# A mixture-of-experts layer: the partial job of an expert moves from first to second place, and the job table takes its sums in two wide operations

## The chip, the core and the metric

The kernel runs on one core of a Trainium2 chip. The metric is the device time of one execution in microseconds (us), over several executions. TensorE (PE in the profile) multiplies matrices, VectorE (DVE), ScalarE (ACT) and GpSimd (POOL) work elementwise, SyncE (SP) only issues transfers here. The engines run on their own and meet at semaphores.

## What is computed

One layer over 1024 latent tokens of width 1024, batch 1: modulation, an input projection, a recurrent head group and a linear-attention head group, an output projection, a normalisation, and then a mixture of 32 experts of which each token takes 4. The change lies in the experts' part. Cut to that, the reference is:

```python
logits = (xt @ w_router + b_router).astype(f32)          # 1024 tokens, 32 experts
top_v, top_i = lax.top_k(logits, 4)
top_w = jax.nn.softmax(top_v, axis=-1)
...
def expert_block(args):                                   # tokens of one expert
    tok, e = args
    xb = xt[tok]
    gate = jnp.minimum(xb @ w_gate[e] + b_gate[e], 7.0)
    up = jnp.clip(xb @ w_up[e] + b_up[e], -7.0, 7.0)
    act = (up + 1.0) * gate * jax.nn.sigmoid(1.702 * gate)
    return act @ w_down[e] + b_down[e]
...
y = jnp.zeros_like(xt).at[row_token].add(y_rows * row_weight)
x = layer_norm(DEEPNORM_ALPHA * x + g2 * y)
```

All is in float32. The weights of an expert are three matrices of 4 MB, 12 MB together; of 32 experts, 384 MB.

## The kernel before, in words

**Jobs.** The 4096 pairs of token and expert are cut, expert after expert, into jobs of at most 128 rows. An expert with NQ quarters of 32 rows has NJ = ceil(NQ / 4) jobs and PAD = 4 NJ - NQ quarters too many. One of its jobs is partial and has the kind 4 - PAD (1, 2 or 3 quarters); the others are of kind 4. The kernel decides this while it runs, from the router's result. It writes a table with one row for each job (lines 1748 to 1773): kind (J_TYP), expert, whether the job is the first of its expert (J_FIRST), and ordinals that say which count of a semaphore to wait for. The table goes to DRAM and back (lines 520 and 522), and every engine reads its rows into registers. Before, the partial job is the first of its expert. Line 1765 gives kind 4 to the very last job of all, whatever its padding, because the end of the kernel is written for that kind.

With the given inputs there are 49 jobs. The counts of matmuls in the timeline of TensorE and the times at which weights are loaded give their kinds, with a bar between experts: 4 4 | 3 | 2 4 | 2 4 | 3 | 1 4 | 2 | 3 | 2 4 4 | 1 | 3 | 2 | 2 4 | 1 | 3 | 4 | 3 | 2 4 4 | 1 4 | 4 | 3 | 3 | 2 | 1 4 | 1 4 4 | 4 | 1 4 | 4 | 4 | 2 4 | 2 4 | 1 4. Jobs are numbered from 0 to 48 and experts from 0 to 31. In the table, job n has row n + 1, and `uf` is the job's number.

**TensorE** (lines 574 to 626 and 964 to 989) runs gate and up of job n (line 586, 64 matmul records for each quarter, 32 columns of the array at a time), then the down projection of job n - 1, then gate and up of job n + 1, and so on. The down projection has a full sweep (line 612) for kind 4, a half sweep (616) for kind 2, a quarter sweep (622) for kind 1, and half and quarter for kind 3. A full sweep takes as long for 29 rows as for 128.

**Weights.** SBUF holds one set: gate and up as four pairs of pieces of 1 MB, down as four pieces. SyncE works through the jobs in order (lines 543 to 566). In its turn for job n it first, if job n + 1 opens an expert, waits until the biases of job n's expert are spread (`bias_spread`, by VectorE at the end of its turn for the job before, line 1703), then issues that expert's biases and its four pairs (line 501), each as soon as gate/up of job n has used the pair. Then, if job n opens an expert, it issues the down row and the down pieces (line 529) of job n's expert, each as soon as the down projection of job n - 1 has used the piece; in a kind-3 job that is in its quarter sweep, which comes last. All these transfers stand in one queue. So the next expert's gate/up weights are loaded from the time at which the expert's last job uses them, and are wanted after the down projection of the job before that one.

**VectorE**, in its turn for job n: it turns the rows of job n + 1 (line 1656), does the swiglu of job n (1684 to 1696), evacuates and weighs the down result of job n - 1 (1638, 1643), turns the activations of job n (1713), and spreads the next biases if an expert ends (1703). **GpSimd** gathers rows (2001) and adds the weighed results into `stream_rows` in DRAM by indirect DMAs (2015).

**The end.** The results of the last three jobs are fetched back separately (`late_rows`, line 2032) and normalised (lines 1669 and 1674), while all other rows are normalised during the last job. The fetch of the last two waits until all scatters before have landed.

Of the kernel before, what the change touches and what calls it, by code (L numbers as in the profile page):

```python
# [13 lines left out]
ALU = mybir.AluOpType  # L14
ACT = mybir.ActivationFunctionType
AX_X = mybir.AxisListType.X
# [4 lines left out]
P = 128  # L21
# [4 lines left out]
class Chain:  # L26
# [5 lines left out]
    def link(self, ins):  # L32
        self.n += 1
        ins.then_inc(self.sem, 1)
        self.eng.wait_ge(self.sem, self.n)


def layer(nc, x, c, ctx, c_ctx, w_ada, b_ada, w_in, conv_w, conv_b, lru_wa, lru_ba, lru_wx, lru_bx,
# [17 lines left out]
    NE, TOPK = w_router.shape[2], 4  # L56
# [12 lines left out]
    J_TYP, J_ORD, J_E, J_FIRST, J_LIVE, J_NJ, J_STORED, J_THREE = range(8)  # L69
# [10 lines left out]
    with ctxs:  # L80
# [104 lines left out]
        tmpO = reg(o, NT, TOPK, NE); o += 1024  # L185
        Gx = reg(o, NT, NE); o += 256
        rt = reg(o, 16, NE); o += 512
# [4 lines left out]
        over = reg(o, NT, NE); o += 256  # L192
# [31 lines left out]
        tabc = small[:, 32:32 + NC].bitcast(I32)  # L224
# [1053 lines left out]
        def _(dve):  # L1278
# [438 lines left out]
            first_slots(NT - 1)  # L1717
            CNT, NQ, NJ, IJ, JS, NN, IO, ON, T0, T1, PAD, N3, I3 = range(13)
            r = lambda i: rt[:, i]
# [4 lines left out]
            def cumulative(dst, src):  # L1724
                link(dve.tensor_tensor_scan(r(dst), r(ON), r(src), 0.0, ALU.mult, ALU.add))
# [17 lines left out]
            link(dve.tensor_scalar(r(NN), r(NQ), 1.0, None, ALU.min))  # L1743
            cumulative(IO, NN)
            link(dve.tensor_scalar(r(N3), r(PAD), 1.0, None, ALU.is_equal))
            cumulative(I3, N3)
# [6 lines left out]
            link(dve.tensor_scalar(r(T0), iot, U[:, 1:2], None, ALU.is_equal))  # L1753
            for i, src in enumerate((JS, PAD, IO, I3)):
                link(dve.tensor_tensor(r(T1), r(T0), r(src), ALU.mult))
                link(dve.tensor_reduce(U[:, 3 + i:4 + i], r(T1), AX_X, ALU.add))
            link(dve.tensor_tensor(U[:, 12:13], uf, U[:, 3:4], ALU.subtract))
            link(dve.tensor_tensor(U[:, 7:8], uf, r(IJ)[:, NE - 1:NE], ALU.is_lt))
            link(dve.tensor_scalar(U[:, 8:9], uf, 0.0, None, ALU.is_ge))
            link(dve.tensor_tensor(U[:, 8:9], U[:, 8:9], U[:, 7:8], ALU.mult))  # L1760
            link(dve.tensor_scalar(U[:, 11:12], U[:, 12:13], 0.0, None, ALU.is_equal))
            link(dve.tensor_tensor(U[:, 9:10], U[:, 11:12], U[:, 4:5], ALU.mult))
            link(dve.tensor_scalar(U[:, 9:10], U[:, 9:10], -1.0, 4.0, ALU.mult, ALU.add))
# [3 lines left out]
            link(dve.tensor_scalar(tabc[:, J_E:J_E + 1], U[:, 1:2], float(NE - 1), None, ALU.min))  # L1767
            link(dve.tensor_scalar(tabc[:, J_ORD:J_ORD + 1], U[:, 5:6], 1.0, 16.0, ALU.max, ALU.mult))
            link(dve.tensor_tensor(tabc[:, J_FIRST:J_FIRST + 1], U[:, 11:12], U[:, 8:9], ALU.mult))
            link(dve.tensor_copy(tabc[:, J_LIVE:J_LIVE + 1], U[:, 7:8]))  # L1770
            link(dve.tensor_copy(tabc[:, J_NJ:J_NJ + 1], r(IJ)[:, NE - 1:NE]))
            link(dve.tensor_scalar(tabc[:, J_THREE:J_THREE + 1], U[:, 6:7], 1.0, 16.0, ALU.max, ALU.mult))
            link(dve.tensor_scalar(tabc[:, J_STORED:J_STORED + 1], uf, 1.0, 16.0, ALU.max, ALU.mult))
# [14 lines left out]
            link(dve.tensor_tensor(over, ranks_, pad_of, ALU.add))  # L1788
            link(dve.scalar_tensor_tensor(out=over, in0=over, scalar=float(P), in1=pad_of, op0=ALU.is_ge, op1=ALU.mult))
            link(dve.scalar_tensor_tensor(out=over, in0=r(JS).unsqueeze(1).to_broadcast([P, NT, NE]), scalar=float(P), in1=over,  # L1790
# [353 lines left out]
```

## Time and profile before

| what | us |
|---|---|
| median of 3 runs | 2292.42 |
| the runs | 2289.76, 2295.86, 2292.42 |
| the profiled execution | 2295.02 |
| its span, first to last instruction | 2293.3 |
| TensorE busy | 2124.1 (93%) |
| VectorE busy | 1000.5 (44%) |
| TensorE on the chain that ended last | 76% of the span |
| expert stage on TensorE, from job 1 on | 718.98 to 2273.6 |

A row of the timeline has the start, the duration, the engine, the line, the operation, what it writes and reads, and how many instructions are merged; in brackets stands how long the engine was idle before it and what ended that. A matmul in float32 leaves two records. A row of waits says who waited for whom: total, times, longest. "To landing" is the time from the issue of a transfer to its completion.

### The profile page before, as it was taken

The numbers are of one execution on the slowest core, as the hardware profiler recorded it, in microseconds if no ns is written. First come the engines' busy times: TensorE is split into PE (matmuls) and PEld (weight loads), VectorE is DVE, ScalarE is ACT, GpSimd is POOL, SyncE is SP. The second block draws the span as 40 slices with busy tenths as digits, with TensorE's granted clock in tenths as the row PEclk, the third lists the DMA queues.
The fourth block names the chain that finished last, engine by engine and source line by source line (L and its number), as shares of the span: only waits on it lengthen the run. The fifth ranks groups of instructions, "written<-read, shape, count | busy, mean of one in ns | idle before, by whom it ended". The sixth has DMA issues, their size and how long they took to land.

```text
span 2293.3 us, 43772 instructions
## 1 busy us (share of the span) xinstructions
PE 2124.1 (93%) x14119; PEld 839.2 (37%) x14120; DVE 1000.5 (44%) x1503; ACT 388.5 (17%) x549; POOL 392.2 (17%) x395
## 2 busy tenths in 40 slices
PE   6999999789958999999997989999998999999995
PEld 3544444554533333332332223333332333333332
DVE  2765655557772332433334242332343333222346
ACT  2343347322210000000000000000000000000023
POOL 1011100202311121222111221311113211212112
PEclk9999999799969999999999999999999999999998
DMA  9222320032245776789479989746899647797683
GB/s 350 84 70 69 101 74 19 1 113 84 83 193 181 288 257 227 290 299 376 139 269 410 356 332 410 285 164 232 306 390 360 223 160 247 267 339 261 213 303 112
DMA packets 153783, 512.29 MB, mean 223 GB/s; under 512 B 17008, under 2 KB 51832, under 8 KB 136203
## 3 DMA queue, kind: packets, MB, share of 16 engines
q1 hardware_dynamic: 136290, 468.96, 53.7%
q0 software_dynamic: 15840, 37.45, 7.6%
q10 hardware_dynamic: 1608, 5.29, 0.6%
q8 instruction: 27, 0.44, 0.1%
q14 instruction: 18, 0.14, 0.0%
HBM read 482.08 MB, written 32.51 MB: 224 GB/s over the span
## 4 chain that ended last, share of the span: by engine, by line
PE 76%; DVE 8%; SPq 6%; DMA 5%; issue 3%; ACT 1%; DVEq 1%; POOLq 0%; ACTq 0%; POOL 0%
PE psall L586 37%; PE psall L612 12%; PE psall L765 9%; PE psall L616 4%; PE psall L753 3%; SPq L501 3%; PE psall L872 2%; PE psall L866 2%; DMA arena<-in_w_down_dram 2%; DMA arena<-in_w_up_dram 2%; PE psall L732 1%; SPq L442 1%; PE psall L622 1%; DVE arena L1483 1%; PE psall L685 1%
## 5 line engine op out<-in xcount | busy, mean ns | idle before, releaser
L586 PE MATMUL psall<-arena 128*32 128x512 f32 x9216 | 1012.3, 598 | 69.3 <-DMA arena<-in_w_up_dram 31.2
L586 PEld LDWEIGHTS psall<-arena 128*32 128x32 f32 x9216 | 299.1, 111 | 770.3 <-issue 770.3
L1656 DVE STREAM_TRANSPOSE arena<-arena 128x1024 f32<-128x1024 f32 x49 | 61.0, 1245 | 726.1 <-PE psall L586 715.2
L612 PE MATMUL psall<-arena 128*128 128x512 f32 x736 | 325.1, 600 | 10.1 <-DVE arena L1638 7.7
L1255 ACT ACTIVATE arena<-arena 128x1024 f32<-128x1024 f32 x49 | 51.8, 1058 | 1362.7 <-DVE arena L1684 1362.7
L765 PE MATMUL psall<-arena 128*128 128x512 f32 (+1 forms) x560 | 227.1, 562 | 0.0
L612 PEld LDWEIGHTS psall<-arena 128*128 128x128 f32 x736 | 139.1, 191 | 196.1 <-issue 192.7
L1638 DVE TENSOR_TENSOR arena<-psall,arena 32x256 f32<-32x256 f32 (+2 forms) x122 | 78.6, 644 | 222.6 <-PE psall L612 172.3
L2001 POOL DMA_INDIRECT arena<-h_rows,lruw x144 | 151.3, 1050 | 82.2 <-POOL lruw L1994 39.3
L765 PEld LDWEIGHTS psall<-arena 128*128 128x128 f32 x560 | 106.3, 190 | 109.1 <-issue 106.1
L616 PE MATMUL psall<-arena 128*64 128x512 f32 x576 | 128.9, 596 | 4.8 <-DMA arena<-in_w_down_dram 4.8
L1994 POOL COPY lruw<-arena 128x4 int32 (+1 forms) x48 | 9.7, 202 | 639.4 <-DVE arena L1656 588.8
L2015 POOL DMA_INDIRECT stream_rows<-arena,lruw x56 | 92.2, 1646 | 93.4 <-DMA stream_rows<-arena,lruw 45.1
L1643 DVE SCALAR_TENSOR_TENSOR arena<-arena,lruw,adarow 32x256 f32<-32x256 f32 (+2 forms) x122 | 85.7, 703 | 6.6
L1255 ACT ACT_TABLE_LOAD x49 | 62.9, 1283 | 80.9 <-issue 80.9
L1713 DVE STREAM_TRANSPOSE arena<-arena 128x1024 f32<-128x1024 f32 (+3 forms) x48 | 74.7, 1557 | 1.6 <-DVE arena L1696 0.5
L616 PEld LDWEIGHTS psall<-arena 128*64 128x64 f32 x576 | 39.9, 137 | 93.1 <-issue 93.1
L2007 POOL COPY lruw<-lruw 128x1 int32 x40 | 8.0, 200 | 382.1 <-DVE arena L1643 351.2
L753 PE MATMUL psall<-arena 128*128 128x512 f32 x160 | 70.0, 592 | 0.0
L1968 POOL TENSOR_TENSOR arena<-arena 128x1280 f32<-128x1280 f32 x8 | 23.3, 2908 | 268.9 <-ACT arena L1080 268.9
L622 PE MATMUL psall<-arena 128*32 128x256 f32 x1024 | 58.8, 380 | 2.6 <-DMA arena<-in_w_down_dram 2.6
L872 PE MATMUL psall<-arena 128*128 128x512 f32 x128 | 59.2, 617 | 0.0
(329 smaller groups left out, 1646.2 us busy)
## 6 DMA issues: line engine op xcount, KB each, us to landing
arena<-in_w_gate_dram SPq DMA_DIRECT2D x128, 1024.0 KB, 7.2
arena<-in_w_up_dram SPq DMA_DIRECT2D x128, 1024.0 KB, 9.4
arena<-in_w_down_dram SPq DMA_DIRECT2D x128, 1024.0 KB, 8.9
arena<-in_w_ada_dram SPq DMA_DIRECT2D x16, 1024.0 KB, 5.3
arena<-in_w_ada_dram SPq DMA_DIRECT2D x4, 2048.0 KB, 14.9
arena<-in_x_dram SPq DMA_DIRECT2D x16, 512.0 KB, 7.1
arena<-in_w_in_dram SPq DMA_DIRECT2D x16, 512.0 KB, 4.1
arena<-in_w_out_dram SPq DMA_DIRECT2D x1, 4096.0 KB, 13.8
```

The lines of the kernel that those rows point to most:

```text
L586: mm = pe.matmul(psGU[QR * j:QR * j + QR, t], xT[:, k, QR * t:QR * t + QR], wpair[m][:, :, k % 2, QW * j:QW * j + QW], start=(k == 0), sto ...
L612: mm = pe.matmul(ps[6 + s], aT[:, k, :], w[:, s * BANK:(s + 1) * BANK], start=(k == 0), stop=(k == KD - 1))
L616: mm = pe.matmul(ps[6][HT * j:HT * j + HT, :], aT[:, k, 0:HT], w[:, j * BANK:(j + 1) * BANK], start=(k == 0), stop=(k == KD - 1), skip_gro ...
L622: mm = pe.matmul(ps[7][QR * j:QR * j + QR, 0:QW], aT[:, k, r], w[:, j * QW:(j + 1) * QW], start=(k == 0), stop=(k == KD - 1), skip_group_c ...
L753: mm = pe.matmul(ps[i % JB][:, :], uT[:, k, j * P:(j + 1) * P], wv[:, k, :], start=(k == 0), stop=(k == KD - 1))
L765: mm = pe.matmul(ps[i % JB][0:w, 0:seg[1] - seg[0]], wring[n % WRING][:, k, 0:w], uT[:, k, seg[0]:seg[1]], start=(k == 0), stop=(k == KD - 1))
L872: mm = pe.matmul(ps[2 * (t % 2) + s][:, :], YT[:, k, t * P:(t + 1) * P], wout[:, k, s * BANK:(s + 1) * BANK], start=False, stop=(k == KD - 1))
L1255: act.activation(sg, gb, ACT.Sigmoid, scale=SWIGLU).then_inc(sg_ready, 1)
L1638: mm = dve.tensor_tensor(yb[p0:p1, c:c + n], psY[p0:p1, c:c + n], ebd[p0:p1, b:b + n], ALU.add)
L1643: mm = dve.scalar_tensor_tensor(out=yb[p0:p1, c:c + n], in0=yb[p0:p1, c:c + n], scalar=(wcolq if c else wcol)[p0:p1], in1=adarow[p0:p1, 3, ...
L2001: pool.indirect_dma_start(out=xg[:, CW * t:CW * (t + 1)], out_offset=None, in_=h2_dram.rearrange("a (j n) -> (a j) n", n=CW), in_offset=ba ...
L2015: return pool.indirect_dma_start(out=to, out_offset=bass.IndirectOffsetOnAxis(ap=index, axis=0), in_=yb[:, cols], in_offset=None, bounds_c ...
```

## The change

The partial job becomes the second of its expert (or the first, if there is only one): a new row JP of the table's arithmetic holds the number of that job, and J_TYP takes the padding there in place of at the first job. The rows are placed accordingly: ranks past 2 x 128 less the padding move on, in place of those past 128 less the padding. The sums that pick an expert's values for each job (JS, PAD, IO, I3) were four multiplies and four reductions over 32 elements; they and JP are now one multiply and one reduction over 5 x 32, for which the rows of `rt` are put in another order. Line 1765 stays.

```diff
-            CNT, NQ, NJ, IJ, JS, NN, IO, ON, T0, T1, PAD, N3, I3 = range(13)
+            CNT, NQ, NJ, IJ, NN, ON, T0, T1, N3, JS, PAD, IO, I3, JP = range(14)
...
             cumulative(IO, NN)
+            link(dve.tensor_scalar(r(T0), r(NJ), -1.0, 1.0, ALU.add, ALU.min))
+            link(dve.tensor_tensor(r(JP), r(T0), r(JS), ALU.add))
...
-            for i, src in enumerate((JS, PAD, IO, I3)):
-                link(dve.tensor_tensor(r(T1), r(T0), r(src), ALU.mult))
-                link(dve.tensor_reduce(U[:, 3 + i:4 + i], r(T1), AX_X, ALU.add))
-            link(dve.tensor_tensor(U[:, 12:13], uf, U[:, 3:4], ALU.subtract))
-            link(dve.tensor_tensor(U[:, 7:8], uf, r(IJ)[:, NE - 1:NE], ALU.is_lt))
+            picks = tmpO.rearrange("p t k e -> p (t k) e")[:, 0:5]
+            link(dve.tensor_tensor(picks, rt[:, JS:JP + 1], r(T0).unsqueeze(1).to_broadcast([P, 5, NE]), ALU.mult))
+            link(dve.tensor_reduce(U[:, 2:7], picks, AX_X, ALU.add))
+            job_js, job_pad, job_io, job_i3, job_jp = (U[:, 2 + i:3 + i] for i in range(5))
+            link(dve.tensor_tensor(U[:, 10:11], uf, r(IJ)[:, NE - 1:NE], ALU.is_lt))
...
-            link(dve.tensor_scalar(U[:, 11:12], U[:, 12:13], 0.0, None, ALU.is_equal))
-            link(dve.tensor_tensor(U[:, 9:10], U[:, 11:12], U[:, 4:5], ALU.mult))
+            link(dve.tensor_tensor(U[:, 11:12], uf, job_js, ALU.is_equal))
+            link(dve.tensor_tensor(U[:, 12:13], uf, job_jp, ALU.is_equal))
+            link(dve.tensor_tensor(U[:, 9:10], U[:, 12:13], job_pad, ALU.mult))
             link(dve.tensor_scalar(U[:, 9:10], U[:, 9:10], -1.0, 4.0, ALU.mult, ALU.add))
             link(dve.tensor_scalar(U[:, 13:14], r(IJ)[:, NE - 1:NE], uf, 1.0, ALU.subtract, ALU.is_equal))
             link(dve.scalar_tensor_tensor(out=U[:, 9:10], in0=U[:, 13:14], scalar=4.0, in1=U[:, 9:10], op0=ALU.mult, op1=ALU.max))
...
-            link(dve.scalar_tensor_tensor(out=over, in0=over, scalar=float(P), in1=pad_of, op0=ALU.is_ge, op1=ALU.mult))
+            link(dve.scalar_tensor_tensor(out=over, in0=over, scalar=2.0 * P, in1=pad_of, op0=ALU.is_ge, op1=ALU.mult))
```

## Rows read from the trace of the kernel before

**Rows 1.** Waits of TensorE, 718 to 2294 us: who, for whom, total, times, longest.

```profile
PE psall L586 <- DMA arena<-in_w_up_dram: 31.2, 15, 4.9
```

**Rows 2.** Timeline of TensorE: parts of jobs without waits, one row for each kind.

```profile
1053.80 7.09 PE L616 MATMUL psall<-arena 128*64 128x512 f32 x32
1128.98 27.67 PE L586 MATMUL psall<-arena 128*32 128x512 f32 x256
1156.58 14.00 PE L612 MATMUL psall<-arena 128*128 128x512 f32 x32
1853.96 27.68 PE L586 MATMUL psall<-arena 128*32 128x512 f32 x256 [1.46 <-issue]
2136.00 13.94 PE L586 MATMUL psall<-arena 128*32 128x512 f32 x128
```

**Rows 3.** Timeline of the end; landings of the last scatter and, from the page, of all.

```profile
2219.47 1.23 DVE L1638 TENSOR_TENSOR arena<-psall,arena 128x1024 f32<-128x1024 f32 x1 [9.14 <-PE psall L612]
2246.85 3.64 PE L622 MATMUL psall<-arena 128*32 128x256 f32 x64
2258.18 15.39 PE L612 MATMUL psall<-arena 128*128 128x512 f32 x32 [7.69 <-DVE arena L1638]
2261.85 2.28 POOL L2015 DMA_INDIRECT stream_rows<-arena,lruw  x1 [0.86 <-POOL lruw L2009]
2276.19 1.28 DVE L1669 SCALAR_TENSOR_TENSOR arena<-arena,lruw,adarow 128x1024 f32<-128x1024 f32 x1
...
DMA to landing us min/median/max: 4.5/4.5/4.5
...
stream_rows<-arena,lruw POOLq DMA_INDIRECT x56, 6.2
```

**Rows 4.** Timeline of TensorE at job 33: start of its gate/up, start of gate/up 34.

```profile
1739.48 3.64 PE L586 MATMUL psall<-arena 128*32 128x512 f32 x32 [1.52 <-issue]
1764.18 27.67 PE L586 MATMUL psall<-arena 128*32 128x512 f32 x256 [0.63 <-issue]
```

**Rows 5.** Timeline of TensorE and SyncE at jobs 18 to 22.

```profile
1254.72 3.64 PE L586 MATMUL psall<-arena 128*32 128x512 f32 x32 [1.64 <-DMA arena<-in_w_up_dram]
1283.60 27.68 PE L586 MATMUL psall<-arena 128*32 128x512 f32 x256 [0.64 <-issue]
1318.22 7.07 PE L586 MATMUL psall<-arena 128*32 128x512 f32 x64
1372.59 29.83 PE L586 MATMUL psall<-arena 128*32 128x512 f32 x256 [4.85 <-DMA arena<-in_w_up_dram]
...
1326.63 0.38 SPq L501 DMA_DIRECT2D arena<-in_w_gate_dram  x1
```

**Rows 6.** Timeline of TensorE at job 12: the first and the last of its pairs.

```profile
1060.82 3.64 PE L586 MATMUL psall<-arena 128*32 128x512 f32 x32
1076.92 5.16 PE L586 MATMUL psall<-arena 128*32 128x512 f32 x32 [2.58 <-DMA arena<-in_w_up_dram]
```

**Rows 7.** SyncE: a burst's first issue; its 18th piece's landing (maximum); all landings.

```profile
1017.14 0.38 SPq L501 DMA_DIRECT2D arena<-in_w_gate_dram  x1
...
L501 SPq DMA_DIRECT2D arena<-in_w_up_dram x1: 2220/2220/2220, 1050.2 to 1050.2; - x1
DMA to landing us min/median/max: 18.7/19.3/19.9
...
DMA to landing us min/median/max: 4.8/8.5/24.2
```

**Rows 8.** Timeline of VectorE at the job table, and TensorE's first row after it.

```profile
653.85 0.37 DVE L1565 TENSOR_REDUCE arena<-arena 128x32 f32<-128x128 f32 x1
663.07 0.19 DVE L1755 TENSOR_TENSOR arena<-arena 128x32 f32<-128x32 f32 x1
664.86 0.16 DVE L1757 TENSOR_TENSOR small<-small 128x1 f32<-128x1 f32 x1
...
673.45 15.81 PE L586 MATMUL psall<-arena 128*32 128x512 f32 x128 [14.09 <-issue]
```

More of the change, by code:

```diff
@@ L1753, in _ @@
             link(dve.tensor_scalar(r(T0), iot, U[:, 1:2], None, ALU.is_equal))
-            for i, src in enumerate((JS, PAD, IO, I3)):
-                link(dve.tensor_tensor(r(T1), r(T0), r(src), ALU.mult))
-                link(dve.tensor_reduce(U[:, 3 + i:4 + i], r(T1), AX_X, ALU.add))
-            link(dve.tensor_tensor(U[:, 12:13], uf, U[:, 3:4], ALU.subtract))
-            link(dve.tensor_tensor(U[:, 7:8], uf, r(IJ)[:, NE - 1:NE], ALU.is_lt))
+            picks = tmpO.rearrange("p t k e -> p (t k) e")[:, 0:5]
[3 more added lines that the diff above has]
+            link(dve.tensor_tensor(U[:, 10:11], uf, r(IJ)[:, NE - 1:NE], ALU.is_lt))
             link(dve.tensor_scalar(U[:, 8:9], uf, 0.0, None, ALU.is_ge))
-            link(dve.tensor_tensor(U[:, 8:9], U[:, 8:9], U[:, 7:8], ALU.mult))
-            link(dve.tensor_scalar(U[:, 11:12], U[:, 12:13], 0.0, None, ALU.is_equal))
-            link(dve.tensor_tensor(U[:, 9:10], U[:, 11:12], U[:, 4:5], ALU.mult))
+            link(dve.tensor_tensor(U[:, 8:9], U[:, 8:9], U[:, 10:11], ALU.mult))
+            link(dve.tensor_tensor(U[:, 11:12], uf, job_js, ALU.is_equal))
+            link(dve.tensor_tensor(U[:, 12:13], uf, job_jp, ALU.is_equal))
+            link(dve.tensor_tensor(U[:, 9:10], U[:, 12:13], job_pad, ALU.mult))
             link(dve.tensor_scalar(U[:, 9:10], U[:, 9:10], -1.0, 4.0, ALU.mult, ALU.add))
@@ L1767, in _ @@
             link(dve.tensor_scalar(tabc[:, J_E:J_E + 1], U[:, 1:2], float(NE - 1), None, ALU.min))
-            link(dve.tensor_scalar(tabc[:, J_ORD:J_ORD + 1], U[:, 5:6], 1.0, 16.0, ALU.max, ALU.mult))
+            link(dve.tensor_scalar(tabc[:, J_ORD:J_ORD + 1], job_io, 1.0, 16.0, ALU.max, ALU.mult))
             link(dve.tensor_tensor(tabc[:, J_FIRST:J_FIRST + 1], U[:, 11:12], U[:, 8:9], ALU.mult))
-            link(dve.tensor_copy(tabc[:, J_LIVE:J_LIVE + 1], U[:, 7:8]))
+            link(dve.tensor_copy(tabc[:, J_LIVE:J_LIVE + 1], U[:, 10:11]))
             link(dve.tensor_copy(tabc[:, J_NJ:J_NJ + 1], r(IJ)[:, NE - 1:NE]))
-            link(dve.tensor_scalar(tabc[:, J_THREE:J_THREE + 1], U[:, 6:7], 1.0, 16.0, ALU.max, ALU.mult))
+            link(dve.tensor_scalar(tabc[:, J_THREE:J_THREE + 1], job_i3, 1.0, 16.0, ALU.max, ALU.mult))
             link(dve.tensor_scalar(tabc[:, J_STORED:J_STORED + 1], uf, 1.0, 16.0, ALU.max, ALU.mult))
```

## The prediction

> **What bounds the kernel now.** I read the page first, then the waits of TensorE in the expert stage, then its timeline there job by job, then SyncE's weight loads and their landings, and last the end of the run. The stage runs from 718.98 to 2273.6 us of a span of 2293.3, two thirds of it, and TensorE is its backbone: its waits on weights are the largest loss (31.2 us for gate/up weights alone) [rows 1], and one wait of 7.7 us stands at the last down projection [rows 3]. Everything else is matmul time. A change of the job order can therefore move two things: what TensorE computes, and where it waits for weights.
>
> The price of a job is read from the starts of neighbouring rows: gate/up of a kind-4 job takes 1156.58 - 1128.98 = 27.60 us, which is the row's 27.67 less 0.07 of overlap, and I take the 0.07 off the others too [rows 2]. Kind 1 is 7.0 [rows 5], kind 2 13.87, kind 3 three quarters of 27.60, 20.7. The down projection takes 13.93 (kind 4) and 7.02 (kind 2) [rows 2], 3.6 (kind 1) [rows 3], and 7.02 + 3.6 = 10.6 (kind 3, both sweeps). After a quarter sweep TensorE loses 1.0 to 1.7 more (1.46 in the row shown). I write gu(n) and down(n) for the two parts of job n; TensorE runs gu(n), down(n-1), gu(n+1), down(n).
>
> **The change part by part.** By J_TYP's new rule the kinds of jobs 0 to 48 become, with a bar between experts:
> 4 4 | 3 | 4 2 | 4 2 | 3 | 4 1 | 2 | 3 | 4 2 4 | 1 | 3 | 2 | 4 2 | 1 | 3 | 4 | 3 | 4 2 4 | 4 1 | 4 | 3 | 3 | 2 | 4 1 | 4 1 4 | 4 | 4 1 | 4 | 4 | 4 2 | 4 2 | 4 4.
> For twelve experts that is the same work in another order. For the last it isn't.
>
> *The last expert, +25.6 us.* It has two jobs, 47 (kind 1) and 48. Line 1765 makes the very last job kind 4 whatever its padding. Before, the short job came first and stayed short. Now the short one would be job 48, which is forced to 4, and job 47 is full: both are kind 4. gu(47) grows by 27.6 - 7.0 = 20.6 us, uncovered, since TensorE has nothing else then. down(47) grows by 10.3, but here there is cover: down(48) began 11.3 us after the end of gu(48) because VectorE had to swiglu, turn and evacuate first (2258.18 - 2246.85, of which 7.7 is the wait) [rows 3]. Now down(47) fills 13.9 of it, the evacuation (L1638, 1.2) and its semaphores follow, and down(48) begins at 15.4 and ends at 29.3, against 26.7 before: +2.7 by TensorE. The other path is the scatter of job 47: evacuation and scaling (1.23 and, as the same shape, 1.3) follow down(47), so it is issued at 13.9 + 2.6 + 1.8 = 18.3 after gu(48), with the 1.8 that POOL took before; before it was 2261.85 - 2246.85 = 15.0. That is +3.3, and the scatter is of 512 KB: the quarter scatter landed in 4.5 us, the median of all 56 is 6.2 [rows 3], +1.7. The rows that wait for it (L2032 fetches them, the normalisation at 2276.19 uses them) were as late as TensorE's before, so the later path counts: +5.0. Bounds for this end part: 2.7 and 6.5. Sum 20.6 + 5.0 = 25.6.
>
> *Job 33, -10.7.* Expert 23's first job was kind 1 and met a queue of weights: from gu(33) at 1739.48 to gu(34) at 1764.18 are 24.7 us, where 7.0 + 7.02 are work [rows 4]. As kind 4 its pairs of weights are wanted 6.9 us apart instead of 1.75, which is slower than they land, and the down weights behind them have 20 us more. All of the 10.7 goes.
>
> *Job 18, -8.0.* Expert 12's first job: 1283.60 - 1254.72 = 28.9 us for 13.87 + 7.02 of work [rows 5]. The same reasoning with kind 4: all 8.0 go.
>
> *Jobs 20 to 22, +5.0.* Expert 12 now ends on the short job. The weights of expert 14 (job 21) are asked for by SyncE only after VectorE has spread the biases at the end of its turn for job 19, and are wanted after gu(20) and down(19). Before: issue at 1326.63, 8.4 us after gu(20) began at 1318.22; wanted at 7.0 + 13.9 = 20.9, so 12.5 us of cover [rows 5]. After: down(19) is 7.0, wanted at 14.0; the issue comes earlier too, since VectorE's turn for a kind-2 job is shorter, at about 6.5. Cover 7.5, that is 5.0 less, on a stretch where the queue is already late (4.85 us of waiting at job 22, 1372.59), so all of it shows. Bounds: 0 if the queue catches up, 9 if it starts with a backlog.
>
> *Job 12, -2.1.* Expert 8's first job was kind 2 and took from 1060.82 to 1082.1, 21.2 us for 13.9: 7.3 lost [rows 6]. As kind 4 it has slack for the later pairs. But expert 5 in front of it now ends on its short job, and that moves a burst. The queue's pace there: the 18th piece of a burst issued from 1017.14 on was issued at 1050.2 and landed 19.9 later, at 1070.1; with 5 us for the first (4.8 is the shortest landing) that is 48/17 = 2.82 us for each piece of 1 MB [rows 7]. After, the burst begins with expert 5's down pieces, when the quarter sweep of down(7) frees them. Back from gu(12), which begins near 1061.6: 2.7 + 1.5 + 7.0 + 0.6 + 13.9 + 13.9 + 3.6 + 1.3 + 20.7 + 7.0 = 72.2, so at 989.4. Expert 8's first pair is complete with the 26th piece: 989.4 + 5 + 25 x 2.82 = 1064.9, a wait of 3.2. Add 1.5 for the lower clock behind such a wait (256 matmuls took 29.83 after a wait of 4.85, against 27.67 [rows 2, 5]) and 0.6 in which down(8) waits for VectorE, which weighs a kind-3 job behind a gate/up of 7.0 only. 5.2 instead of 7.3. Bounds: -7.3 and +2.
>
> *Elsewhere 0.* The other short second jobs free 8 MB of weights within 7 or 14 us, and TensorE has a full down projection of 13.9 before it wants the first pair: 21 us. In that time four down pieces and two of gate/up land, 6 x 2.82 + 2.2 = 19.1. Cover is left, but it is 2 us. The pattern of kind 4, a quarter sweep and kind 1, behind which TensorE waits for VectorE, stands once in either order (down(34) before, down(35) after).
>
> By the Trainium skill ("DMA: Bandwidth & Descriptors", "Anatomy of one DMA") the moving part of a transfer is its bytes over 436 GB/s, 2.4 us for such a piece; an estimate by it would put the 26th piece 10 us earlier, take the wait at job 12 away and make the sum about 5 us lower. The trace's 2.82 is with POOL's gathers and scatters in between, and the page's "Issuing engines are not separate DMA queues" says that these interleave on the same engines; the measured pace decides.
>
> *The job table, -0.6.* Eight links from 663.07 to 664.86 go, 0.224 us each, 1.79 in all [rows 8]. Instead come one multiply and one reduce over 160 elements, which I take at 0.4 each with their link (a reduce over 128 took 0.37), and two small links, 0.44 together: 1.24. TensorE stood idle 14.1 us until the table was in (673.45), so 0.6 is on the path. Bounds 0 and -0.9. The other edits swap one small operation for another.
>
> Sum: 25.6 - 10.7 - 8.0 + 5.0 - 2.1 - 0.6 = +9.2 us. The profiled execution took 2295.02 us (span 2293.3), so 2304.2 for it; the median of the runs is 2292.42, 2.6 lower, so 2301.6.
>
> **The rivals.** *The waits go and don't come back.* The whole answer hangs on the queue's pace. If pieces land at 2.70 or faster, the 26th piece at job 12 is in time: -7.3 instead of -2.1; and at jobs 20 to 22 eight pieces are in a microsecond earlier and the queue catches up, +1 instead of +5. Then 25.6 - 10.7 - 8.0 + 1 - 7.3 - 0.6 = 0, and with the end at its lower bound -2.3: 2290 to 2292, not slower. For it: within a burst neighbouring pieces come 2.5 us apart (5.0 a pair). Against: the 48/17 above.
>
> *New waits behind the short second jobs.* The cover of 21 us against 19.1 is thin. If the pace is 3.2 at such a place, because a gather and a scatter fall into it, 21.4 is needed, and with the clock's 1.5 four or five places (experts 5, 18, 23, 24, 26) give some 2 each: +10, 2311. For it: the stretch from job 12 to job 22 runs at the queue's limit already. Against: at most of these places the down pieces land before the burst.
>
> *The last job is not made longer* (some other rule keeps job 47 at 32 rows): without the 25.6 the rest gives 2276. Against it stands line 1765, which takes the maximum with 4 for the last job, and the new JP, which for two jobs is the second.
>
> **How the numbers follow.** The forecast has 0.64, waits gone 0.20, new waits 0.12, last job not longer 0.04. The range reaches from 2294 (the forecast with job 12 at -7.3 and the end at its lower bound, toward the first rival) to 2311 (the second rival). A measurement of this kernel can tell about 0.3%, 6.9 us, from no change: slower means above 2299.3. Of the forecast's own spread about a sixth lies below that. Slower 0.52 + 0.12 = 0.64; faster than 2285.5 the last rival and a little of the first, 0.06; the same 0.30.
>
> **What would show it.** In the profile after: 147 quarter groups of gate/up instead of 144 (L586 with 9408 matmuls of 9216), L612 with 32 more and L622 with 64 fewer; gu(47) with 256 matmuls of 27.7 us, and down(48) some 15 us behind gu(48) without the 7.7 us wait; gu(33) and gu(18) unbroken; a wait near 3 us ahead of gu(12), and a longer one ahead of gu(21); eight operations fewer of L1755 and L1756. If job 47 is short, or if gu(12) and gu(21) start without waits, the sum is wrong by the terms above.

## The result and the profile after

| | before | after |
|---|---|---|
| median, us | 2292.64 of 4 runs | 2309.64 of 4 runs |
| lowest and highest | 2289.76 and 2295.86 | 2308.79 and 2309.80 |
| the profiled execution | 2295.02 | 2309.80 |
| its span | 2293.3 | 2308.1 |
| gate/up matmul records (line 586) | 9216 | 9408 |

The ratio is 1.0073, with a 95% interval from 1.0056 to 1.0091: slower, by 17.0 us in the medians and 14.8 in the profiled executions. The forecast was 2301.6, with slower as the likeliest verdict and a range of 2294 to 2311 that holds the time. The sum for the profiled execution was +9.2, so it fell short by 5.6. One run of e1 below, 2365.23 us at a granted clock of 0.923 where its others have 0.967 to 0.971, is left out of its median.

From the page of the changed kernel, its groups of gate/up and full down matmuls (form and count, then busy time and mean ns, then idle time before them), and three of its waits of TensorE from 716 us on (who, for whom, total, times, longest):

```profile
L586 PE MATMUL psall<-arena 128*32 128x512 f32 x9408 | 1035.7, 597 | 58.4 <-issue 28.3
L612 PE MATMUL psall<-arena 128*128 128x512 f32 x768 | 337.7, 598 | 5.6 <-issue 3.8
...
PE psall L586 <- DMA arena<-in_w_up_dram: 20.9, 9, 4.9
PE psall L586 <- issue: 14.8, 14, 2.3
PE psall L612 <- issue: 3.8, 1, 3.8
```

The 192 additional records are the three quarters that the last expert gained; the full down projections have 768 records, 32 more than before. The waits on gate/up weights fell from 31.2 us in 15 places [rows 1] to 20.9 in 9. So the waits fell, and more was lost at the end.

TensorE's timeline at the places that the prediction names, jobs 11 and 12, 21, 33, and the end from job 47 on:

```profile
1035.95 5.62 PE L586 MATMUL psall<-arena 128*32 128x512 f32 x48 [1.43 <-DMA arena<-in_w_up_dram]
1068.74 29.05 PE L586 MATMUL psall<-arena 128*32 128x512 f32 x256 [3.16 <-DMA arena<-in_w_up_dram]
...
1337.75 7.05 PE L586 MATMUL psall<-arena 128*32 128x512 f32 x48 [2.32 <-issue]
...
1738.13 27.67 PE L586 MATMUL psall<-arena 128*32 128x512 f32 x256 [1.67 <-issue]
1765.73 7.09 PE L616 MATMUL psall<-arena 128*64 128x512 f32 x32
1772.75 7.07 PE L586 MATMUL psall<-arena 128*32 128x512 f32 x64
...
2192.03 27.67 PE L586 MATMUL psall<-arena 128*32 128x512 f32 x256
2219.63 7.09 PE L616 MATMUL psall<-arena 128*64 128x512 f32 x32
2226.65 27.67 PE L586 MATMUL psall<-arena 128*32 128x512 f32 x256
2254.25 14.00 PE L612 MATMUL psall<-arena 128*128 128x512 f32 x32
2272.01 15.67 PE L612 MATMUL psall<-arena 128*128 128x512 f32 x32 [3.76 <-issue]
```

The first row of gate/up 33 answers to [rows 4], where the same job was cut into pairs; now it runs unbroken. Gate/up 12 still waits, 3.16 us in place of several waits [rows 6]. Gate/up 47 (at 2192.03) has 256 records, not 64. The down projection in front of the last gate/up takes 7.09 us, and the last down projection begins 17.8 us after the end of the last gate/up (2272.01 - 2254.25), against 11.3 before [rows 3]. Behind the end of that gate/up the span goes on for 53.85 us, before for 46.45.

VectorE at the job table:

```profile
665.20 0.33 DVE L1757 TENSOR_TENSOR arena<-arena 128x160 f32<-128x160 f32 x1
665.56 0.32 DVE L1758 TENSOR_REDUCE small<-arena 128x5 f32<-128x160 f32 x1
665.91 0.16 DVE L1760 TENSOR_TENSOR small<-small,arena 128x1 f32<-128x1 f32 x1
...
674.52 1.08 PE L586 MATMUL psall<-arena 128*32 128x512 f32 x4 [13.47 <-issue]
```

The two wide operations take 0.71 us with their links (665.91 - 665.20), where eight small ones took 1.79 [rows 8], and TensorE's idle time ahead of its first gate/up fell from 14.09 to 13.47 us.

### The profile page after: what moved, and what is told of

It reads as the page before. It is cut to its first block, busy times and chain, and to the rows that moved or that the text cites. A ratio compares the mean times of both kernels' runs of the same rounds, so it can differ in the third digit from the quotient of the medians.

```text
span 2308.1 us, 44095 instructions
## 1 busy us (share of the span) xinstructions
PE 2158.0 (93%) x14279; PEld 861.9 (37%) x14280; DVE 1005.5 (44%) x1493; ACT 388.5 (17%) x549; POOL 394.4 (17%) x398
## 4 chain that ended last, share of the span: by engine, by line
PE 78%; DVE 7%; SPq 5%; DMA 5%; issue 3%; ACT 1%; DVEq 0%; POOLq 0%; ACTq 0%; POOL 0%
PE psall L586 38%; PE psall L612 13%; PE psall L765 9%; PE psall L616 4%; PE psall L753 3%; DMA arena<-in_w_up_dram 3%; PE psall L872 2%; PE psall L866 2%; SPq L501 2%; PE psall L732 1%; PE psall L622 1%; SPq L442 1%; DVE arena L1483 1%; PE psall L685 1%; DMA arena<-stream_rows 1%
## 5 line engine op out<-in xcount | busy, mean ns | idle before, releaser
L586 PE MATMUL psall<-arena 128*32 128x512 f32 x9408 | 1035.7, 597 | 58.4 <-issue 28.3
L586 PEld LDWEIGHTS psall<-arena 128*32 128x32 f32 x9408 | 317.5, 111 | 764.7 <-issue 762.3
L612 PE MATMUL psall<-arena 128*128 128x512 f32 x768 | 337.7, 598 | 5.6 <-issue 3.8
L612 PEld LDWEIGHTS psall<-arena 128*128 128x128 f32 x768 | 144.5, 191 | 199.1 <-issue 194.6
L2004 POOL DMA_INDIRECT arena<-h_rows,lruw x147 | 154.8, 1053 | 83.1 <-POOL lruw L1997 39.2
L765 PEld LDWEIGHTS psall<-arena 128*128 128x128 f32 x560 | 106.3, 190 | 109.1 <-issue 106.1
L753 PE MATMUL psall<-arena 128*128 128x512 f32 x160 | 70.0, 592 | 0.0
L872 PE MATMUL psall<-arena 128*128 128x512 f32 x128 | 59.3, 617 | 0.0
L866 PE MATMUL psall<-arena 128*128 128x512 f32 x128 | 57.0, 598 | 1.6 <-DVE arena L1606 1.6
## 6 DMA issues: line engine op xcount, KB each, us to landing
arena<-in_w_out_dram SPq DMA_DIRECT2D x1, 4096.0 KB, 13.9
```

Of the source, the lines that this page charges most:

```text
L586: mm = pe.matmul(psGU[QR * j:QR * j + QR, t], xT[:, k, QR * t:QR * t + QR], wpair[m][:, :, k % 2, QW * j:QW * j + QW], start=(k == 0), sto ...
L612: mm = pe.matmul(ps[6 + s], aT[:, k, :], w[:, s * BANK:(s + 1) * BANK], start=(k == 0), stop=(k == KD - 1))
L753: mm = pe.matmul(ps[i % JB][:, :], uT[:, k, j * P:(j + 1) * P], wv[:, k, :], start=(k == 0), stop=(k == KD - 1))
L765: mm = pe.matmul(ps[i % JB][0:w, 0:seg[1] - seg[0]], wring[n % WRING][:, k, 0:w], uT[:, k, seg[0]:seg[1]], start=(k == 0), stop=(k == KD - 1))
L866: pe.matmul(ps[2 * (t % 2) + s][:, :], YT[:, k, t * P:(t + 1) * P], wout[:, k, s * BANK:(s + 1) * BANK], start=(k == 0), stop=False)
L872: mm = pe.matmul(ps[2 * (t % 2) + s][:, :], YT[:, k, t * P:(t + 1) * P], wout[:, k, s * BANK:(s + 1) * BANK], start=False, stop=(k == KD - 1))
```

## The experiments

**How they were made.** In all kernels but two, the table of the changed kernel is used with one more row M, 1 for each expert whose partial job is to come second and 0 for the others. The number of the partial job is JS + min(NJ - 1, M), and the ranks move on accordingly. With M = 0 everywhere the job order is that of before. For expert 8 alone the lines are these, with one second memset for each chosen expert:

```diff
+            link(dve.memset(r(M), 0.0))
+            link(dve.memset(r(M)[:, 8:9], 1.0))
...
-            link(dve.tensor_scalar(r(T0), r(NJ), -1.0, 1.0, ALU.add, ALU.min))
+            link(dve.scalar_tensor_tensor(out=r(T0), in0=r(NJ), scalar=-1.0, in1=r(M), op0=ALU.add, op1=ALU.min))
...
-            link(dve.tensor_tensor(over, ranks_, pad_of, ALU.add))
-            link(dve.scalar_tensor_tensor(out=over, in0=over, scalar=2.0 * P, in1=pad_of, op0=ALU.is_ge, op1=ALU.mult))
+            link(dve.scalar_tensor_tensor(out=r(T1), in0=r(M), scalar=-float(P), in1=r(PAD), op0=ALU.mult, op1=ALU.add))
+            link(dve.tensor_tensor(over, ranks_, r(T1).unsqueeze(1).to_broadcast([P, NT, NE]), ALU.add))
+            link(dve.scalar_tensor_tensor(out=over, in0=over, scalar=float(P), in1=pad_of, op0=ALU.is_ge, op1=ALU.mult))
```

**How they are compared.** The traces differ by several microseconds before the experts even begin: down(0) begins between 744 and 749 us in them. So a difference at one place is taken between two jobs, after subtracting what the two traces differ by at down(0). Each kernel has one trace, and traces with the same job order still differ at single places: e4 by up to 1.7 us from before, and e1 by 2.5 from e2 at gate/up 37, where the two kernels are still in the same order. A difference below that, read from one pair of traces, is not shown. "The end" is the time from the end of the last gate/up to the end of the span.

| run | partial job second for | median, us | ratio to before, 95% | span | the end |
|---|---|---|---|---|---|
| changed kernel | all | 2309.64 | 1.0056 to 1.0091 | 2308.1 | 53.85 |
| e4 | none | 2292.15 | 0.9989 to 1.0009 | 2290.7 | 47.36 |
| e3 | the last, 31 | 2319.23 | 1.0093 to 1.0128 | 2317.0 | 51.59 |
| e5 | 30 | 2301.18 | 1.0029 to 1.0057 | 2295.8 | 53.43 |
| e1 | all but 31 | 2285.65 | 0.9945 to 0.9976 | 2289.3 | 52.48 |
| e2 | all but 30, 31 | 2280.16 | 0.9931 to 0.9959 | 2277.5 | 48.57 |
| e6 | 5 | 2300.37 | 1.0024 to 1.0052 | 2295.6 | 46.98 |
| e8 | all but 5, 30, 31 | 2274.95 | 0.9915 to 0.9942 | 2275.6 | 47.23 |
| e7 | 8, 12, 23 | 2280.85 | 0.9944 to 0.9972 | 2278.6 | 46.66 |
| e9 | 8, 12, 23, 24 | 2270.70 | 0.9883 to 0.9913 | 2273.9 | 47.29 |
| e10 | all, biases spread early | 2296.04 | 1.0003 to 1.0021 | 2294.8 | 53.96 |
| e11 | all, two row groups normalised late | 2311.33 | 1.0058 to 1.0085 | 2312.0 | 55.96 |
| e12 | 8, 12, 23, 24, biases early | 2261.66 | 0.9840 to 0.9876 | 2261.4 | 45.32 |

### The last two experts: e1 to e4

Edits: M = 1 for all but 31 (e1), for all but 30 and 31 (e2), for 31 alone (e3), for none (e4). In the texts on record, theory A puts all that is lost on the last expert; theory B puts only the longer gate/up there, and some 7 us on expert 30, whose short second job (7.09 us of down projection in place of 14.00) now stands in front of the last gate/up.

> The change, but expert 31, the last, keeps its partial job first (a mask over the experts; same result). Theory A (the end's whole cost belongs to the last expert's two full jobs): job 47 is of kind 1 again, so all that the end added in the trace of after goes, 20.6 us of gate/up and 7.4 behind the end of gu(48), 28 in all: 2309.6 - 28 = 2281.6. Theory B (of the 7.4 most belongs to expert 30, whose partial job 46 now comes second: down(46) is 7.0 us instead of 14.0, the loading of the stream rows for the last normalisation starts behind swiglu(47) as before, and VectorE reaches swiglu(48) 8.7 us after gu(48) instead of 1.8): only the 20.6 go and at most 1 more, 2309.6 - 21 = 2288.6, and the wait ahead of the last down projection grows to some 14 us.

> As the run before, and expert 30 keeps its partial job first as well. Theory A: no change against the run before, 2281.6 in both. Theory B: here the whole 28 us go, about 2281.6, 7 us less than the run before; the last down projection begins some 11.3 us after the end of gu(48), as in the kernel before, with a wait near 7.7.

> The kernel before with the wide table sums, and only expert 31 has its partial job second. Theory A: +28 us, 2320.6. Theory B: gate/up 20.6, and at the end what the forecast worked out for a full down(47) alone, 2.7 to 5.0: +23.3 to +25.6, 2316 to 2318; down(48) begins about 15.4 us after gu(48) ends.

> The kernel before with the wide table sums alone (every expert has its partial job first; a mask that is zero). All theories: no difference that a time can show, -0.6 us; in the trace TensorE's idle time ahead of the expert stage is about 13.5 us instead of 14.1, from which this kernel's extra memsets take nothing, since they stand in a wait. The order of the jobs is that of before, so the waits on weights at jobs 12, 18, 22 and 33 stand as before: this is also the base for the runs that move one expert.

Measured: e1 took 2285.65 us (its runs reach from 2280.31 to 2290.97), e2 2280.16, e3 2319.23, e4 2292.15. TensorE's rows of the last two down projections in e1 and then in e2:

```profile
2236.82 3.66 PE L622 MATMUL psall<-arena 128*32 128x256 f32 x64
2253.05 16.46 PE L612 MATMUL psall<-arena 128*128 128x512 f32 x32 [12.58 <-DVE arena L1638]
```

```profile
2228.93 3.64 PE L622 MATMUL psall<-arena 128*32 128x256 f32 x64
2240.84 16.96 PE L612 MATMUL psall<-arena 128*128 128x512 f32 x32 [8.28 <-DVE arena L1638]
```

The time of e1 alone lies between the two theories; the trace decides. With expert 30 turned back the last down projection waits 8.28 us, not 12.58, the end is 3.9 us shorter (52.48 - 48.57), and the medians are 5.5 us apart. e3 against e4 is +27.1 in the medians and +26.3 in the spans: 20.6 of it is the longer gate/up, 4.2 the end (51.59 - 47.36), 1.3 a difference that the traces have before down(0), and 0.2 lies between. The forecast gave the last expert 25.6, and e3 bears out its steps too. TensorE's last two down projections and the scatter of job 47 in e3:

```profile
2265.41 14.00 PE L612 MATMUL psall<-arena 128*128 128x512 f32 x32
2280.78 13.97 PE L612 MATMUL psall<-arena 128*128 128x512 f32 x32 [1.36 <-issue]
...
2283.50 1.63 POOL L2021 DMA_INDIRECT stream_rows<-arena,lruw  x1 [0.86 <-POOL lruw L2013]
```

The last down projection begins 15.4 us after the last gate/up (2280.78 - 2265.41), as forecast, and the scatter is issued 18.1 us after it, for the forecast's 18.3. So the price of the last expert was right; e2 shows an additional one at expert 30, which e3 does not have. e4 shows that the table costs and gains nothing that the medians can tell.

### Expert 30 alone: e5

Edit: M = 1 for expert 30.

> The table of the changed kernel; the partial job comes second for expert 30 alone (kinds 4 2 in place of 2 4), the last expert keeps 1 4. Compared with the table-only kernel (2292.15 us, span 2290.7). Theory B (the job before the last two is what delays the end): down(46) takes 7.1 us in place of 14.0, so the last gu ends 7 us earlier after the loads of stream rows that are issued behind the Sigmoid of job 47; with the 22.9 us from their landing to L1684 in the changed kernel's trace, and landings 12 to 16 us after issue, L1684 begins 4.9 to 8.7 us behind the last gu in place of 1.8, and down(48) starts 3 to 7 us later after it: 2295 to 2299 us, idle before down(48) 14 to 18 us in place of 11 to 12. Theory A (the end lengthens only with the last expert's own jobs): 2292.2 us, no change at down(48).

Measured: 2301.18 us, a little above theory B; the profiled execution, at 2297.5 the fastest of its five, lies within it. The wait ahead of the last down projection is 14.39 us, the end is 6.1 us longer than in e4 (53.43 - 47.36):

```profile
2242.37 3.64 PE L622 MATMUL psall<-arena 128*32 128x256 f32 x64
2260.40 15.68 PE L612 MATMUL psall<-arena 128*128 128x512 f32 x32 [14.39 <-DVE arena L1638]
```

The reason stands on ScalarE and VectorE. ScalarE fetches all stream rows (line 1234) behind the Sigmoid of job 47, takes eight row statistics and only then gives the Sigmoid of job 48; VectorE normalises six groups of 128 rows ahead of the swiglu of job 48. The changed kernel's rows of ScalarE (Sigmoid 47, the fetch, Sigmoid 48) and VectorE (swiglu 48):

```profile
2222.28 1.06 ACT L1255 ACTIVATE arena<-arena 128x1024 f32<-128x1024 f32 x1 [38.40 <-DVE arena L1684]
2224.18 6.13 ACTq L1234 DMA_DIRECT2D arena<-stream_rows  x8
2265.46 1.06 ACT L1255 ACTIVATE arena<-arena 128x1024 f32<-128x1024 f32 x1
...
2262.95 1.22 DVE L1684 TENSOR_TENSOR arena<-psall,arena 128x1024 f32<-128x1024 f32 x1
```

VectorE is free for the swiglu 38.8 us after the fetch is issued, ScalarE for the Sigmoid 41.3 us after. The fetch stands at a fixed place behind gate/up 47, and behind that come down(46) and the last gate/up. With down(46) 7 us shorter, the last gate/up ends 7 us earlier relative to the fetch. Expert 30 alone and the last expert alone cost 6.1 and 4.2 us at the end; together, in the changed kernel, they cost 6.5 more than e4 and not 10.3. Both delay the same down projection, which fits the overlap.

### Normalising two row groups later: e11

Edit, in the changed kernel, in VectorE's turn for the last job:

```diff
-                                        for T in range(4, 6):
-                                            normalise(T)
...
                                     by_kind(dve, tp, lambda kind: weigh(u, kind, orderp))
+                                    with dve.If(typ_of(dve, typ_n) < 1):
+                                        ch.n = chained + 4
+                                        for T in range(4, 6):
+                                            normalise(T)
```

> The changed kernel as it is (2309.64 us, span 2308.1), but VectorE normalises stream rows 4 and 5 (L1660 to L1665) behind the weighing of job 47 in place of ahead of swiglu(48). Theory (they hold swiglu(48) back to 8.7 us after the last gu, and with it down(48), which starts 17.8 us after it in place of the 15.4 forecast): L1684 of swiglu(48) about 3 to 4 us after the last gu, down(48) 15.4 us after it, the end 2.4 us earlier: span 2305.7, about 2307 us. Rival (the scatter of job 47 behind them sets the end): down(48) starts earlier but the span stays at 2308, 2309 to 2310 us.

Measured: 2311.33 us of 5 runs from 2307.25 to 2313.78, no gain that the runs can tell. VectorE in e11 (the swiglu's first and last operation and its transpose), and ScalarE's Sigmoid:

```profile
2260.07 1.23 DVE L1684 TENSOR_TENSOR arena<-psall,arena 128x1024 f32<-128x1024 f32 x1 [1.99 <-issue]
2268.15 1.23 DVE L1696 SCALAR_TENSOR_TENSOR arena<-arena 128x1024 f32<-128x1024 f32 x1 [3.66 <-ACT arena L1255]
2269.41 2.01 DVE L1707 STREAM_TRANSPOSE arena<-arena 128x1024 f32<-128x1024 f32 x1
2290.62 1.23 DVE L1652 TENSOR_TENSOR arena<-psall,arena 128x1024 f32<-128x1024 f32 x1 [0.19 <-DVE lruw L1649]
...
2267.06 1.06 ACT L1255 ACTIVATE arena<-arena 128x1024 f32<-128x1024 f32 x1
```

The swiglu did begin 4.0 us after the last gate/up (2260.07 - 2256.04) in place of 8.7, but then it waited 3.66 us for the Sigmoid, which was behind ScalarE's own eight statistics. The last down projection begins 16.7 us after the last gate/up, not the 15.4 expected. And the four normalisations that were left for later hold up the last evacuation (2290.62, 2.5 us after the down projection ends at 2288.1), so the end is 2.1 us longer than in the changed kernel (55.96 - 53.85). The theory on record was half right: VectorE was one of two engines behind the same late fetch, and freeing one moves the wait to the other. Whether an earlier fetch would help is not shown: no run moves it.

### Expert 5, and what a burst waits for: e6, e8, e10

Up to gate/up 15 the changed kernel has 0.4 us more than before, where the forecast has -2.1. Its trace shows waits at gate/up 10 and 11 that nothing forecast. Edits: M = 1 for expert 5 alone (e6) and for all but 5, 30 and 31 (e8); in e10 the changed kernel spreads the biases right behind the swiglu:

```diff
                             by_kind(dve, typ_of(dve, typ_c), lambda kind: swiglu(u, kind))
+                            with dve.If(dve.snap(first_n, min_val=0, max_val=1) > 0):
+                                spread_bias(ord_of(dve, ord_n, wait_p))
...
-                            with dve.If(dve.snap(first_n, min_val=0, max_val=1) > 0):
-                                spread_bias(ord_of(dve, ord_n, wait_p))
```

> The table of the changed kernel; the partial job comes second for expert 5 alone (jobs 8 and 9 are 4 1 in place of 1 4); job 12 keeps kind 2. Compared with the table-only kernel (2292.15 us, span 2290.7). Theory B (the missing 2.6 us at jobs 10 to 16 come from expert 5): VectorE's weigh(8) waits about 12.8 us and expert 7's burst of DMA issues comes at about 1026 in place of 1017 us, so gu(10) and gu(11) wait 2 to 3 us in all, and gu(12) still waits its 5 us or more: 2294 to 2297 us. Rival (the burst's place is set by job 12's own order, or the late burst is hidden): burst at about 1017, gu(10) and gu(11) without waits, 2292 us.

> The partial job second for all experts but 5, 30 and 31, against the kernel with all but 30 and 31 (2280.16 us). If expert 5 costs the 2.6 us missing at jobs 10 to 16: about 2277.5 us, expert 7's burst at about 1017 us again, and no waits at gu(10) and gu(11). If it does not: 2280 us.

> The changed kernel as it is (2309.64 us, span 2308.1), but VectorE spreads the next expert's gate and up biases (L1703) directly behind the swiglu of a job, ahead of its weighing of the down projection; SyncE issues an expert's biases and gate/up pieces only after that spread. Theory (the stalls at jobs 10 to 12 come from the burst that expert 5's new order moved behind the full down(8)): the biases of expert 7 are issued at about 1010 in place of 1024.5 us, the waits of gu(10), gu(11) and gu(12), about 7 us with their clock, go, and the cover at jobs 20 to 22 grows by the length of a turn: 2296 to 2302 us. Rival (the pace of the landings is the limit, the issue is not): bursts are issued earlier but land no earlier where TensorE waits, 2307 to 2310 us.

Measured: e6 2300.37 us, above what was expected: from down(0) to gate/up 15 it is 7.2 us longer than e4, with a wait of 2.24 ahead of gate/up 11, where e4 has none, and of 7.4 in all at gate/up 12, where e4 has 5.3. The rest stands in gate/up 11, which takes 22.4 us in place of 20.7, at a granted clock of 0.93 from 1030 to 1056 us. A burst is what SyncE issues for one expert: its biases and its eight gate/up pieces. The first bias and the first piece of expert 7's burst, in e4 and then in e6:

```profile
1013.82 0.59 SPq L534 DMA_DIRECT2D arena<-in_b_gate_dram  x1
...
1015.33 0.38 SPq L501 DMA_DIRECT2D arena<-in_w_gate_dram  x1
```

```profile
1020.15 0.59 SPq L534 DMA_DIRECT2D arena<-in_b_gate_dram  x1
...
1021.67 0.38 SPq L501 DMA_DIRECT2D arena<-in_w_gate_dram  x1
```

and in e10, with TensorE's start of gate/up 10 (the job whose pairs that burst replaces):

```profile
1008.93 0.59 SPq L534 DMA_DIRECT2D arena<-in_b_gate_dram  x1
1017.74 0.38 SPq L501 DMA_DIRECT2D arena<-in_w_gate_dram  x1
1027.94 2.36 SPq L501 DMA_DIRECT2D arena<-in_w_up_dram  x1
...
1012.43 1.07 PE L586 MATMUL psall<-arena 128*32 128x512 f32 x8
```

e10 took 2296.04 us, which is the lower edge of the theory's range, but not by the theory's route: it refutes the cause at this place. The biases went out at 1008.93 in place of 1024.51 (4.0 us of it is a difference that the trace has from down(0) on), but the weights didn't follow: their first pair is free only when gate/up 10 has used it, and gate/up 10 begins at 1012.43. The last pair was issued at 1027.94, which after those 4.0 us is as late as the 1031.73 of the changed kernel. The waits ahead of gate/up 11 and 12 are 0.91 and 3.15 us, in the changed kernel 1.43 and 3.16. So at this place the order of TensorE's own work decides. In e4 gate/up 10 begins at 1003.47 and has the full down(9) of 14 us behind it; in e6 it begins at 1011.56 and has a down(9) of 3.64 us behind it. Expert 7's weights are asked for later and wanted as early as ever: the same loss of cover that the prediction had priced at jobs 20 to 22, and missed here.

Where the 13.6 us between the medians of e10 and the changed kernel come from, the profiles show in two other stretches: 6.6 us from gate/up 15 to gate/up 18 and 3.5 up to gate/up 22 (gate/up 21 starts without its 2.32 us). From down(0) to the end the two traces differ by 9.3 us. The other 4.0 stand ahead of down(0), where the edit does nothing, so 9.3 is the surer number. In those two stretches the first pair was already free, and SyncE waited for VectorE's spread: its first piece is issued 11.2 us after gate/up 16 begins (1205.17 - 1194.00) and in e10 5.9 (1195.07 - 1189.12), and 6.2 us after gate/up 20 begins (1327.55 - 1321.34) and in e10 2.1 (1312.60 - 1310.48).

e8 took 2274.95 us, 5.2 less than e2. Job 12 kept its full gain: 7.5 us between gate/up 12 and gate/up 15, against e4. But a new wait came up ahead of it, in the half sweep of down(7), 2.75 us in three pieces, and 3.7 with what follows from it:

```profile
962.14 1.94 PE L616 MATMUL psall<-arena 128*64 128x512 f32 x8 [0.44 <-DMA arena<-in_w_down_dram]
964.75 1.94 PE L616 MATMUL psall<-arena 128*64 128x512 f32 x8 [0.68 <-DMA arena<-in_w_down_dram]
968.32 1.94 PE L616 MATMUL psall<-arena 128*64 128x512 f32 x8 [1.63 <-DMA arena<-in_w_down_dram]
```

Expert 3 ends on a short job there and expert 5 begins with one: down(6) takes 7.09 us and gate/up 8 takes 7.07, and the down weights of job 7 are asked for during the one and wanted behind the other. If all experts have the same order, one of the two is long: gate/up 8 takes 27.6 us in e2, and down(6) 13.9 in e4.

### Only the experts that waited: e7 and e9

Edits: M = 1 for experts 8, 12 and 23, whose first job waited for weights before (e7); and for 24 too (e9).

> The table of the changed kernel; the partial job comes second for experts 8, 12 and 23 alone: those whose partial job waits for its weights in the trace of before (jobs 12, 18 and 33). Compared with the table-only kernel (2292.15 us, span 2290.7). Theory: each gain belongs to its own expert: -2.1 to -7.3 at job 12, -8.0 at job 18, +2.7 given back at jobs 20 to 22, -10.7 at job 33: 2269 to 2274 us, the best version. Rival: the gains need the neighbours' new order or are given back (as the pace of the weights sets the time): the sum is no better than the -12 us of the kernel with all experts but the last two, 2280 us.

> The table of the changed kernel; the partial job second for experts 8, 12, 23 and 24, that is the kernel of experts 8, 12 and 23 (2280.85 us, span 2278.6) with the neighbour behind job 33 turned too. Theory (the 10.7 us that expert 23 frees are kept only where expert 24, behind it, begins with a full job and not with a quarter job that needs all eight of its pieces within 7 us): the waits of 3.2 and 5.5 us in gu(35) go, and this kernel ends 10 to 12 us earlier, 2267 to 2271 us. Rival (the pace of the weights sets the time from job 33 on, and the waits turn up behind job 36 instead): 2278 to 2281 us.

Measured: e7 2280.85 us, which is the rival's number. Its gains are there: from down(0) on it is 7.3 us ahead of e4 at gate/up 15 and 10.5 at gate/up 23. But behind job 33 stands this:

```profile
1725.16 27.68 PE L586 MATMUL psall<-arena 128*32 128x512 f32 x256 [1.67 <-issue]
...
1787.71 1.92 PE L586 MATMUL psall<-arena 128*32 128x512 f32 x16 [3.23 <-DMA arena<-in_w_up_dram]
1795.16 3.64 PE L586 MATMUL psall<-arena 128*32 128x512 f32 x16 [5.53 <-DMA arena<-in_w_up_dram]
```

Gate/up 33 is unbroken, and gate/up 35, the quarter job with which expert 24 begins, waits 8.76 us in two places. Before, the pairs of expert 24 were asked for over the 27.6 us of a full gate/up 34. Now gate/up 34 is the short one (1759.78), all eight pieces are asked for within 7.2 us (1764.76 to 1771.95), and they are wanted from 1780.71 on within another 7. This is the prediction's rival of new waits behind the short second jobs; in the changed kernel it stays away, where the job behind is a full one. e9 turns expert 24 too. Gate/up 35 is then a full job, its waits are gone, and from gate/up 34 to gate/up 38 it takes 12.0 us less than e7. 2270.70 us against 2280.85: within what the theory gave.

### The best version: e12

Edit: e9 with the early spread of e10.

> The kernel with the partial job second for experts 8, 12, 23 and 24 (2270.7 us) with VectorE's spread of the next expert's biases directly behind the swiglu. Theory (the spread is what holds the bursts back at jobs 15 to 17 and 20 to 22, where the early spread took 6.0 and 3.5 us off the changed kernel, and that does not hang on the order of expert 5 or of the last experts): 9 to 10 us less, 2259 to 2263 us, and the wait ahead of gu(17) near 1.4 us in place of 5.1. Rival (the early spread only gave back what the changed order had cost): 2268 to 2271 us.

Measured: 2261.66 us, 1.4% under before, as expected. The row of gate/up 17 in e9 and then in e12:

```profile
1218.47 5.70 PE L586 MATMUL psall<-arena 128*32 128x512 f32 x32 [5.07 <-DMA arena<-in_w_up_dram]
```

```profile
1210.72 3.64 PE L586 MATMUL psall<-arena 128*32 128x512 f32 x32 [1.43 <-issue]
```

From gate/up 15 to gate/up 23 the early spread takes 10.6 us off e9 and took 10.0 off the changed kernel (9.0 and 13.6 in the medians), so it does not repair what the change had done: it is one instruction group that stood behind an unrelated wait.

## Why the prediction was right, and where it was short

*The sign and the main term.* The last expert was forecast at 25.6 us. Gate/up 47 grew by 20.6, as forecast. The end grew by 7.4 (53.85 - 46.45) in place of 5.0, and outside the bound of 6.5. e3 has the last expert's part alone: 4.2 against e4, inside the bounds of 2.7 and 6.5, with the last down projection and the scatter where the forecast had them. What failed is a step that is not there: expert 30 was counted among those with "the same work in another order", and that order takes 7 us of down projection from the place that covered the fetch of the stream rows. e5 shows it at 6.1 us by itself.

*Job 33, -10.7.* Measured from gate/up 33 to gate/up 34: all of it went. The reasoning holds only with the neighbour: e7 gives all of it back by gate/up 38 (10.4 us ahead of e4 at gate/up 33, 10.0 at gate/up 38), 8.8 as waits at job 35 and more with the clock, 0.86 granted from 1780 to 1803.8 us. The prediction had no sentence on expert 24. It was right because the change turned that expert too. Another 2.4 us went at jobs 34 to 37 in this pair of traces (0.9 against the trace of e4), which was not forecast and is no more than the traces differ by.

*Job 18, -8.0.* Measured -8.0. *Jobs 20 to 22, +5.0.* Measured +2.7 in this pair of traces, inside the bounds of 0 and 9; the issue came at 1327.55 and gate/up 21 waited 2.32, 0.63 and 0.85 us. More traces put it nearer the forecast. From gate/up 18 to gate/up 23 the old order takes 159.5, 158.2, 158.1 and 157.6 us (before, e4, e3, e5) and the new one 154.2, 156.2, 155.1 and 154.8 (changed kernel, e11, e1, e2). The means differ by -3.3, which with the -8.0 leaves +4.7.

*Job 12, -2.1.* The wait ahead of gate/up 12 was forecast at 3.2 and measured at 3.16, but by a wrong route. The working let expert 5's down pieces begin a burst at 989.4 and run on without a gap, so that only the 26th piece was late. In fact expert 7's pairs were issued from 1026.01 on, behind gate/up 10. Jobs 10 and 11 waited too, and the stretch gained nothing: +0.4 from down(0) to gate/up 15, and +1.4 between the means of the four traces of each order named above. Single experts show the two halves: expert 8 alone takes 7.3 us away (e7), expert 5 alone adds 7.2 (e6). The prediction let expert 5 keep 5.2 of expert 8's 7.3 us, all of them at job 12, and had nothing for jobs 10 and 11.

*Elsewhere 0.* Between gate/up 15 and gate/up 18 the changed kernel lost 2.3 us more, at jobs 16 and 17. No run isolates it, but it recurs: e1, e2 and e11, with the same order there, lost 2.4 to 2.6 against before, and between the means of the four traces of each order it is 1.8. e10 shows that this stretch hangs on the time at which the biases are spread.

*The table, -0.6.* Measured -0.62 in TensorE's idle time (14.09 - 13.47); in the median of e4 it can't be told.

The sum: 20.6 + 7.4 at the end, and -13.2 before it, where the forecast has -16.4. In the -13.2 are 1.5 us by which the two traces differ at down(0), so the jobs themselves have -14.7. That is the +14.8 measured in the profiles. The medians differ by 2.2 us more, since the profiled execution of before lay 2.4 above its median. That the time lies in the range is in part luck: the missing step at expert 30 (2.4), jobs 10 to 12 (2.5) and jobs 15 to 17 (2.3) all went against the forecast, and jobs 20 to 22 and 34 to 37 took 2.3 and 2.4 of it back in this pair of traces.

*The rivals.* "The waits go and don't come back" (2290 to 2292) fell: they came back at jobs 10, 11 and 21. "New waits behind the short second jobs" (2311) has the nearer number, and its mechanism was at work at one of the five experts it named, expert 5, where it cost 7 us and not 2. "The last job is not made longer" fell with the 9408 records.

On the Trainium skill: the prediction set the trace's 2.82 us for a piece against an estimate of 2.4 us, worked out from the rate on the page "DMA: Bandwidth & Descriptors" ("Anatomy of one DMA"). What failed at jobs 10 to 12 was neither number but the start of the burst: expert 7's weights were issued late, which a pace does not contain.

## What to carry to other kernels

Reordering work that loads its own weights moves two times: when a buffer is free, and how much work stands between that and the first use. Price both at every place where the work between changes, not only where a wait is seen now; a stall that is removed alone can turn up again at the next short piece of work, as in e7, and leaves only when that neighbour is turned too. Ask of the end of a kernel what the last jobs were covering: fetches and statistics for the epilogue can hang on the length of a job two places ahead. And before reordering, look at what gates the issue of the loads: moving one bias spread ahead of an unrelated wait brought 9.0 us in the medians with one order, and 13.6 with the other, of which the traces place 9.3 behind down(0).

## What the runs showed of the hardware

An operation of VectorE over five times the elements cost little more: the multiply over 128x160 took 0.33 us and the reduction 0.32, where the multiply over 128x32 took 0.19 [rows 8]. An estimate from the two multiplies: 128 more elements in a row cost 0.14 us, so 32 cost some 0.035, and some 0.15 of the 0.19 us are not its elements.

A kind-3 job scatters twice, and the kernel lets the second scatter wait until the first has landed. How long that is the trace of e10 shows: the second scatter of job 7 was issued at 1007.31, 8.6 us after the first at 998.68, of which 6.97 was that wait. No run leaves the wait out.

```profile
998.68 1.66 POOL L2018 DMA_INDIRECT stream_rows<-arena,lruw  x1 [1.54 <-issue]
1007.31 1.59 POOL L2018 DMA_INDIRECT stream_rows<-arena,lruw  x1 [6.97 <-DMA stream_rows<-arena,lruw]
```
